# Seven of the eight products of the state space layer's gated unit as three part products, with splits kept in memory the recurrence has finished with

## The reference, cut to what matters

```python
def s5_glu(h, lam_re, lam_im, log_dt, b_re, b_im, c_re, c_im, d_skip, w_glu, b_glu):
    ...
    _, ys = lax.scan(chunk_step, state0, u)
    y = jnp.moveaxis(ys, 0, 1).reshape(Bsz, S, D_MODEL).astype(h.dtype)
    z = jax.nn.gelu(y) @ w_glu + b_glu
    return z[..., :D_MODEL] * jax.nn.sigmoid(z[..., D_MODEL:])
```

## Time and profile before

| | before |
|---|---|
| median of 3 runs | 2018.98 us (2018.93 to 2019.34) |
| the profiled execution, its own time | 2018.36 us |
| its span in the profile | 2016.6 us |
| TensorE busy | 1890.2 us, 94% of the span |
| VectorE busy | 1331.1 us, 66% |
| ScalarE busy | 1082.7 us, 54% |
| granted TensorE clock, mean | 0.968 |
| read from memory | 406.22 MB, 202 GB/s over the span |

### The profile page before, as it was taken

How to read it: one execution, slowest core, us unless ns; L and a number is a source line. 1 busy time by engine, 2 the same in 40 slices (tenths; PEclk the granted TensorE clock), 3 DMA queues, 4 the chain that set the end, 5 groups by cost and what they waited for, 6 DMA issues and landing times.

```text
span 2016.6 us, 31044 instructions
## 1 busy us (share of the span) xinstructions
PE 1890.2 (94%) x12786; PEld 1669.8 (83%) x12786; DVE 1331.1 (66%) x1779; ACT 1082.7 (54%) x1601; POOL 10.4 (1%) x12
## 2 busy tenths in 40 slices
PE   7998899999999998999899899997999979899996
PEld 5887677777777768999788799986999868799995
DVE  3625999999999986555434466543678694366542
ACT  3334888988888875343334443433544462344432
POOL 0000000000000000000000000000000020000000
PEclk9998999999999999999999899998999978899998
DMA  6325899999999993553143355423597211454410
GB/s 248 126 91 201 326 368 357 366 365 357 362 360 367 361 374 128 188 188 137 63 135 128 156 195 188 176 86 125 203 106 261 101 44 64 165 209 179 173 74 21
DMA packets 56482, 409.40 MB, mean 203 GB/s; under 512 B 15360, under 2 KB 20992, under 8 KB 22160
## 3 DMA queue, kind: packets, MB, share of 16 engines
q1 hardware_dynamic: 51792, 400.51, 55.1%
q10 hardware_dynamic: 4544, 6.85, 1.1%
HBM read 406.22 MB, written 1.11 MB: 202 GB/s over the span
## 4 chain that ended last, share of the span: by engine, by line
PE 70%; DVE 25%; ACT 3%; issue 1%; DMA 0%; ACTq 0%; DVEq 0%; SPq 0%
PE wk L1566 25%; DVE ws_moe L1050 16%; PE acc L1544 13%; PE wk L359 8%; PE wk L1004 3%; PE wk L1825 3%; PE wk L365 2%; PE wk L928 2%; PE acc L894 2%; PE acc L711 1%; DVE rstd L286 1%; PE wk L314 1%; PE acc L1854 1%; DVE sq L1117 1%; DVE xp_moe L1072 1%
## 5 line engine op out<-in xcount | busy, mean ns | idle before, releaser
L1050 DVE TENSOR_TENSOR ws_moe<-ring,ws_moe 128x1024 fp32r<-128x1024 f32 x384 | 447.4, 1214 | 5.4 <-ACT ws_moe L1043 5.2
L1043 ACT ACTIVATE ws_moe<-ring 128x1024 fp32r<-128x1024 f32 x384 | 384.3, 1051 | 5.5 <-PE wk L1004 2.2
L1566 PE MATMUL wk<-hx,gu 128*128 128x256 f32 x2112 | 277.0, 289 | 4.8 <-DVE hx L1582 4.5
L1566 PEld LDWEIGHTS wk<-hx,gu 128*128 128x128 f32 x2112 | 265.7, 195 | 10.0 <-DVE hx L1582 6.7
L1004 PE MATMUL wk<-ws_moe,xp_moe 128*128 128x512 f32 x1024 | 268.1, 404 | 1.6 <-DVE xp_moe L1072 1.6
L1544 PE MATMUL acc<-hh_ffn,dn_ffn 128*128 128x256 f32 x2112 | 267.1, 283 | 0.0
L1566 PE MATMUL wk<-hx,gu_ffn 128*128 128x256 f32 x2112 | 260.6, 283 | 0.0
L1544 PEld LDWEIGHTS acc<-hh_ffn,dn_ffn 128*128 128x128 f32 x2112 | 259.5, 192 | 0.0
L1566 PEld LDWEIGHTS wk<-hx,gu_ffn 128*128 128x128 f32 x2112 | 256.6, 192 | 0.0
L1518 ACT ACTIVATE hT<-hT 128x256 f32<-128x256 f32 x88 | 36.8, 419 | 364.0 <-DVE hT L1599 364.0
L1004 PEld LDWEIGHTS wk<-ws_moe,xp_moe 128*128 128x128 f32 x1024 | 187.1, 188 | 43.4 <-issue 2.8
(11 more groups left out here) (341 smaller groups left out, 2217.9 us busy)
## 6 DMA issues: line engine op xcount, KB each, us to landing
ring<-in_u_moe SPq DMA_DIRECT2D x129, 1536.0 KB, 8.5
ring<-in_u_ffn SPq DMA_DIRECT2D x88, 1536.0 KB, 6.6
ring<-in_u_qkv SPq DMA_DIRECT2D x12, 1024.0 KB, 4.9
ring<-in_u_ple SPq DMA_DIRECT2D x8, 1280.0 KB, 5.5
ring<-in_u_in SPq DMA_DIRECT2D x9, 1024.0 KB, 4.9
ring<-in_u_glu SPq DMA_DIRECT2D x8, 1024.0 KB, 4.9
ring<-in_u_out SPq DMA_DIRECT2D x4, 1024.0 KB, 4.8
ring<-in_u_o SPq DMA_DIRECT2D x4, 1024.0 KB, 4.8
```

Source lines behind the costliest of these rows:

```text
L1043: e.activation(WS[:, n % NWS, 0, :], piece(x), ACT.Copy).then_inc(s.m_hi, 1)
L1050: e.tensor_tensor(WS[:, n % NWS, 1, :], piece(x), WS[:, n % NWS, 0, :].bitcast(F32), SUB).then_inc(s.m_lo, 1)
L1566: m = e.matmul(b[:, a * T:(a + 1) * T], gu_of(c, f)[:, x, a * 1024 + k * 128:a * 1024 + (k + 1) * 128], HX[:, y, k, :], start=k == 0 and a ...
```

## The change

Unit gate 0 is multiplied as before, in plain fp32. The seven others (value 0 to value 3, numbered 1 to 7 in the new code) are multiplied as three fp32r matmuls each, 48 to a unit. For this,

- ScalarE copies each of the seven weight units into a high part of type fp32r (`glu_hi`), and VectorE subtracts it for the low part (`glu_lo`), each in one instruction of 128x2048;
- odd units use `GU0`, units 2, 4 and 6 the area `gu`, unit 7 two thirds of the area `dn`. Unit 1's copy waits for the last drives, units 2 and 7 for the last states of the recurrence; the others wait until the unit before last has been multiplied;
- ScalarE copies each pair of tiles after its GELU into the high part of `HX` (4 instructions of 128x512), VectorE makes the low part (4 of 128x512);
- a slot of the ring is given back when the low part has been made (`w_lo`), not when the products are done, for units 1 to 7;
- before the first tile of the next network is split into `GU0`, ScalarE waits until unit 5 has been multiplied.

Some names of signals that nothing used are dropped.

```diff
@@ plan_ssm
             for u in range(4):
                 K.then(("gate", u), ("val", u))
-                load(("gate", u), A["u_glu"][2 * u], 2048, (s.filled, K("gate", u) + 1))
-                load(("val", u), A["u_glu"][2 * u + 1], 2048, (s.filled, K("val", u) + 1))
+                for n, x in ((2 * u, "gate"), (2 * u + 1, "val")):
+                    load((x, u), A["u_glu"][n], 2048, (s.w_lo, w_parts("glu") + n) if n else (s.filled, K(x, u) + 1))
@@ new
+        GLU = [(x, u) for u in range(4) for x in ("gate", "val")]
+
+        def glu_w(n):
+            gu, dn, _ = ffn_area[3]
+            if n == 7:
+                return [dn[:, i, :, :].rearrange("p a n -> p (a n)") for i in range(2)]
+            return [(GU0 if n % 2 else gu)[:, i, :] for i in range(2)]
+
+        def glu_hi(e, n):
+            if n == 1:
+
+                e.wait_ge(s.vfull, NQ)
+            elif n == 2 or n == 7:
+
+                e.wait_ge(s.drive, NQ)
+            else:
+                e.wait_ge(s.filled, K(*GLU[n - 2]) + 1)
+            arrived(e, GLU[n])
+            e.activation(glu_w(n)[0], tile(GLU[n]), ACT.Copy).then_inc(s.w_hi, 1)
+
+        def glu_lo(e, n):
+            hi, lo = glu_w(n)
+            e.wait_ge(s.w_hi, w_parts("glu") + n)
+            e.tensor_tensor(lo, tile(GLU[n]), hi.bitcast(F32), SUB).then_inc(s.w_lo, 1)
+
+        def glu_pe(e, n):
+            b = bank_in(e, K(*GLU[n]))
+            e.wait_ge(s.w_lo, w_parts("glu") + n)
+            hl = glu_w(n)
+            for k in range(8):
+                if n == 1:
+                    e.wait_ge(s.x_lo, x_parts("glu") + k // 2 + 1)
+                for a in range(2):
+                    for i, (x, y) in enumerate(THREE):
+                        m = e.matmul(b[:, a * T:(a + 1) * T], hl[x][:, k * 256 + a * 128:k * 256 + a * 128 + 128], HX[:, y, k, :],
+                                     start=k == 0 and a == 0 and i == 0, stop=k == 7 and i == 2, skip_group_check=True)
+            m.then_inc(s.filled, 1)
@@ ssm_act
             for m in range(2, NQ):
                 tables_act(e, m)
                 decay_act(e, m)
+            glu_hi(e, 1)
             for j in range(4):
                 e.wait_ge(s.y_, 2 * j + 2)
                 e.activation(hT[:, 2 * j:2 * j + 2, :], sq[:, 2 * j:2 * j + 2, :], ACT.Gelu_apprx_tanh).then_inc(s.gelu, 1)
+                e.wait_ge(s.gelu, j + 1)
+                e.activation(HX[:, 0, 2 * j:2 * j + 2, :], hT[:, 2 * j:2 * j + 2, :], ACT.Copy).then_inc(s.x_hi, 1)
+            glu_hi(e, 2)
@@ ssm_act, in the loop over u behind the two sigmoids
                 m.then_inc(freed[k % 4], 1)
+                for n in (2 * u + 3, 2 * u + 4):
+                    if n < 8:
+                        glu_hi(e, n)
+
+            e.wait_ge(s.filled, K("val", 2) + 1)
             ffn_early_act(e, 3)
@@ ssm_pe
-            for u in range(4):
-                arrived(e, ("gate", u))
-                feature_major(e, K("gate", u), by_k(tile(("gate", u))), hT,
-                              new=(lambda t: e.wait_ge(s.gelu, t // 2 + 1)) if u == 0 else None)
-                arrived(e, ("val", u))
-                feature_major(e, K("val", u), by_k(tile(("val", u))), hT)
+            arrived(e, ("gate", 0))
+            feature_major(e, K("gate", 0), by_k(tile(("gate", 0))), hT, new=lambda t: e.wait_ge(s.gelu, t // 2 + 1))
+            for n in range(1, 8):
+                glu_pe(e, n)
             sums_pe(e, "z")
@@ ssm_dve
             for k in range(NQ - 3, NQ):
                 skip(k)
+            glu_lo(e, 1)
+            for j in range(4):
+                e.wait_ge(s.x_hi, x_parts("glu") + j + 1)
+                e.tensor_tensor(HX[:, 1, 2 * j:2 * j + 2, :], hT[:, 2 * j:2 * j + 2, :], HX[:, 0, 2 * j:2 * j + 2, :].bitcast(F32),
+                                SUB).then_inc(s.x_lo, 1)
+            glu_lo(e, 2)
             for u in range(4):
+                if u < 3:
+                    glu_lo(e, 2 * u + 3)
                 bank_read(e, K("gate", u))
@@ ssm_dve, in the same loop behind the two products of the value
                 m.then_inc(freed[k % 4], 1)
+                if u < 2:
+                    glu_lo(e, 2 * u + 4)
             ffn_early_dve(e, 3)
```

More of the change, by code:

```diff
@@ L80, in __call__, with __init__, then @@
         return self.place[name if len(name) > 1 else name[0]]
+class Tally:
+    def __init__(self):
+        self.base, self.n = {}, 0
+    def then(self, name, n):
+        self.base[name], self.n = self.n, self.n + n
+    def __call__(self, name):
+        return self.base[name]
 class Scr:
@@ L107 @@
     "E gl_in gl cum expN glc expE mixed vz S P nrm qz gm "
-    "logits wrg xg rc gex gexd e2 e2d M flag late h2 sel m_hi m_lo m_used m_gl m_fold m_sil m_act m_tr m_mh m_mhl "
+    "wrg xg rc gex gexd e2 e2d M flag sel m_hi m_lo m_used m_gl m_fold m_sil m_act m_tr m_mh m_mhl "
     "m_last m_yl m_y m_gat m_xh m_xl m_gt m_G m_comb m_shift "
     "f_gh f_gl f_dh f_dl f_xh f_xl f_xs f_g f_s f_p f_hh f_hl f_dn f_end "
-    "ple_y "
-    "rvec rv lamt lame zq q2 kf V S2 P2 o2 o2n "
+    "x_hi x_lo w_hi w_lo ple_y "
+    "rv lamt lame zq S2 P2 o2 o2n "
     "ld_cb ld_cc ld_e ld_bt4 ccz dtx tB rx fr sn ab abw ld_ri eB eX cw cX cX3 cb cbd tab rm th W drive y_ gelu vfull vfree "
-    "b_filled b_inv b_cT b_pick b_row b_sil b_hid b_dn b_end"
+    "b_filled b_inv b_pick b_sil b_hid b_dn b_end"
 ).split()
@@ L202, in program @@
                    ("ffn_out", 3), ("ple", 1), ("ple_out", 1))
+        x_parts, w_parts = Tally(), Tally()
+        x_parts.then("glu", 4)
+        w_parts.then("glu", 7)
         g_at = Order()
```

## The result

The changed kernel takes 2007.02 us (median of 4 runs, 2006.56 to 2007.44), the kernel before 2019.16 beside it (4 runs, 2018.93 to 2023.44). The ratio is 0.9940, with a 95% interval of 0.9926 to 0.9953. Measured again beside other kernels, it took 2007.96 (5 runs, 2006.99 to 2008.77) and the kernel before 2017.52 (9 runs, 2016.33 to 2021.00): ratio 0.9950, 0.9936 to 0.9963. So the change wins 0.4 to 0.7%, 10 to 12 us. The forecast was 2009.3, with a range down to 2007.2: the direction is right, the first median lies 0.2 us outside the range, and the second, 2007.96, inside it.

A forecast was written before the change was run, and what follows sets the result against it. TensorE's work bounds the gated unit, holding 70% of the chain. Products 8.03 plus clock 1.7 save 9.7 us from 2018.36, giving 2008.7; with 0.62 for the median, 2009.3 us, range 2007.2 to 2012.2.

The forecast's parts named there:

- The products: Gated unit on TensorE: seven units at 5.76 us instead of 6.907, as in the network behind, gain 8.03 us.
- The first hand-over: Work due before unit 1, while unit 0 runs: fits with 0.9 us slack, cost 0, range 0 to 1 us.
- The splits between units: Signal, copy, gap, subtraction and signal between units: 4.87 us under 5.76, slack 0.9 us, cost 0.
- The ring: Weight loads for units 6, 7 and the next network's first tiles come earlier: cost and gain 0.
- The clock: Behind the layer, work moves 8 us earlier: one of two short pauses behind the network keeps full clock, gain 1.7 us.
- both are kept: Rival: both short pauses behind the network keep the clock, 8.03 + 3.2 = 11.2 us saved, 2007.8 us; chance 0.22.
- later return: At the network's start: clock returns 1.2 us later relative to the work, 0.6 us more lost.
- The median: Whole kernel: the median of the runs stands 0.62 us above the profiled execution, giving 2009.3 from 2008.7.
- the thin cover: Rival, splits between units: copies and subtractions 30% to 60% slower, saved 2 to 7 us, 2012 to 2017; chance 0.10.
- the slower case: Rival, gated unit: both splits take twice their time, 7.41 us a unit, 6 us slower, 2025; chance 0.03.

## Why the prediction was right or wrong

- **The products, 8.03 us: right.** 5.76 us a unit, seven times, 8.02 in the stage, and 8.05 (55.36 - 47.31) with the clock taken out. A product takes 0.120 us here as in the network. The 109 ns that the prediction sets against this was not seen, and it was the wrong figure to set there. The Trainium skill (TensorE: Matmul & The Clock Gate, "Back-to-back issue gap") gives that formula for an isolated matmul, and says itself that it misses the rate of a stream of weight loads and matmuls.
- **The first hand-over, 0: right.** Unit 1 starts at 1691.61 with gate 0 at 1684.79, 6.82 us later, and no wait is put down to VectorE. The low parts of the activations were done at 1687.91 + 2.49 = 1690.4, 1.2 us ahead where I had 0.9. One reading was wrong: the first GELU comes not 7 us later than before but 3.8, counted from gate 0 (1680.00 and 1684.79 against 1676.98 and 1685.58). It cost nothing either way.
- **The splits between units, 0: right,** with a slack of 1.2 us where I had 0.9. The chain is 4.58 us instead of 4.87: the first signal takes 0.20 and not 0.3, the gap 0.03 and not 0.13, the last signal 0.15 and not 0.25.
- **The ring, 0: right.**
- **The clock, 1.7 us: this is the term of the sum that was mis-sized.** I took one of the two short pauses as kept. Both were, 3.16 us in the traces, less 0.55 lost at the network's start, together 2.6 (the table's 2.7 with 0.08 of small differences). The rival "both are kept" had a chance of 0.22, but it had nothing lost at the start; that later return I had priced, at 0.6, only for the other end. The mechanism was the right one, but my reason for choosing one of the two, that the shorter pause is nearer to the one that costs nothing, was no measurement: with 20 products more the pause of 2.08 us loses the clock and the longer one of 2.96 keeps it. The pause of 2.08 us keeps it 260.68 us behind gate 0 and loses it at 261.02.
- **The median, 0.62 us above the profile: not a constant.** Gate 0 starts anywhere within 3.7 us in profiles of programs that are alike up to there, and medians of the kernel before range from 2017.52 to 2019.16. I had nothing for that in the range, and 0.2 us were missing at its end. Of the 2.2 us between the forecast and the first median, 1.0 is the clock's term (10.71 - 9.7). Another 0.7 is that gate 0 happened to start 0.79 earlier, less 0.07 outside the span, and 0.5 that the median stood 0.09 above the profiled execution and not 0.62. These last two are luck: in the second measurement gate 0 starts at 1686.67. With the clock's term right, the forecast would have been 2008.3, and the two medians lie 1.3 and 0.3 us below that.
- Of the rivals, the thin cover and the slower case did not come about. Two experiments bring them about in other ways than the rivals had it: 2.4 us in the stage with subtractions twice as long, and 22 us slower than before with one area, where I had expected 12. With one area the pauses bring the clock down as well, and that was in no price of mine.

## What to carry to other kernels

Count a product's gain from the stage that already runs it, in the same shapes, and count the hand-over chain against the unit's time; both held here within 0.3 us. Whatever moves TensorE's pauses in time can also change what the clock makes of them, by 1.5 to 1.7 us a pause here, so a change of a few microseconds should be judged with the pauses filled, or from the traces stage by stage. Filling TensorE's pauses with products whose results are overwritten gave more here, 13.4 us in the changed kernel and 14.9 in the one before, than the 8.0 of the change by itself.

## What the runs showed of the hardware

- The same pause of 2.08 us, ahead of the same 32 records, is followed by full speed (7.14 us) or by a stretch at half (8.83). It kept the clock where it began 260.34, 260.38 and 260.68 us behind the start of gate 0, and lost it at 261.02, 261.61 and 261.63, in one profile each.
- The length of a short pause doesn't decide: with 20 products more one of 2.07 us lost the clock and one of 2.96 kept it.
- More added work can cost less: 20 products 2.92 us, 10 products 3.84.
- Pauses of 4.42 us between bursts of 48 products made each burst 1.4 to 2.7 us longer.
- Behind 16 filling products a pause of 2.04 us was left. In the kernel before, the clock fell 0.8 us into the work behind it; in the changed kernel's profile, with 2.03 us, it didn't. A gap left open after filling can still cost, and one profile doesn't tell whether it does.
